# Seven mixer projections of a fused two-model block as split high and low products, with three weight slots instead of four

## The chip, the cores and the metric

The kernel runs on one core of a Trainium2 chip. The metric is the device time of one execution in microseconds (us). The program is written engine by engine: each engine has an instruction stream of its own, executes it strictly in order, and meets the others only through semaphores.

## The reference

The reference computes, for 256 tokens of width 1024, one block with a mixer and a retrieval layer, and then a two-layer model on its result. Only the start of it matters here:

```python
h = _rmsnorm(x, norm1_g[l])
p = h @ w_in[l]
(gq, gk, gv, gz, ga, gb, mq, mk, mv, mo, mi, mf) = jnp.split(p, offsets, axis=-1)
y_a = _gdn_group(gq, gk, gv, gz, ga, gb, conv_w[l], gdn_a_log[l], gdn_dt_bias[l], gdn_norm_g[l])
y_b = _mlstm_group(mq, mk, mv, mo, mi, mf, mlstm_i_bias[l], mlstm_f_bias[l], mlstm_norm_g[l])
```

`h @ w_in` is a 256 x 1024 by 1024 x 4128 product in float32. Its 4096 columns beside the gates are eight blocks of 512: the queries, keys and values of the gated delta rule (`gq`, `gk`, `gv`, which go through a five-tap convolution and a SiLU, and the first two through a normalisation), its output gate, and the queries, keys, values and output gate of the mLSTM. The delta rule inverts a triangular matrix per 128 tokens, head and direction. After the block comes a retrieval layer that gathers rows of two tables, and then a second model with modulated norms; the modulation (`ada`) is a product of one conditioning vector with a 50 MB matrix.

## The kernel before

**Projections.** The eight column blocks are called `proj(0)` to `proj(7)`, in the order keys, values, queries of the delta rule, then mLSTM values, mLSTM queries, mLSTM keys, delta-rule gate, mLSTM gate. Each has a weight block `("in", n)` of 1024 x 512 (2 MB, `slots[i]`, [128, 4096]). The normalised input lies transposed in `hT` ([128, 8, 256]: eight chunks of the width, 256 tokens). A projection is two groups `g`, each filling one PSUM bank of 512 columns; a group is two accumulations of eight matmuls of 128x128 by 128x256, except `proj(3)`, where it is one accumulation of eight matmuls with 512 columns and the tokens as output rows. Operands are float32. The profile shows each such float32 matmul as two records, so a projection of 32 matmuls stands there as 64, and `proj(3)` with 16 as 32.

**The order on TensorE** is written out by hand: gates, `proj(0)`, the cumulated gates (`cum`, and after a wait for VectorE's `v_cc` their transposes `crow`), `proj(1)`, `em`, `proj(2)`, `l2(1,0)` (sums of squares of the keys), `decays(0)`, `decays(1)`, `l2_rows(1,0)` (waits for `v_rq`), `proj(3)`, `decays(2)`, `decays(3)`, the key products `kk`, `proj(4)`, `l2(0,1)`, `tokens(0)`, `l2_rows(0,1)`, `proj(5)`, the query products `kq` with two steps of `cond` between, `proj(6)`, `tokens(1)`, `proj(7)`, then for four heads a step of `cond` and four transposes `dd`, and then `level(1..6)`, each level with eight steps, and behind each step one of `cond` and one of `mlstm`.

**PSUM** is a ring of seven banks. `take(name, reader, n)` waits until the bank's last reader is done. So `proj(4)` waits for `v_at0` 3, VectorE's product in `decays(2)`, and `tokens(0)` waits for `v_kk` 1, VectorE's first product with `kk`.

**The order on VectorE**: normalised input, gates (`v_gl`), cumulated gates (`v_cc`), `v_crow` and scans (`v_rows`), `conv(1,0)` (16 multiply-adds), `em`, `conv(2,1)`, `l2_root(1,0)`, `decays(0)`, `decays(1)`, `l2(1,0)`, `conv(0,2)`, `decays(2)`, `decays(3)`, `l2_root(0,1)`, four `kk` products, `l2(0,1)`, four `kq` products, four first blocks of `DT`.

**The order on ScalarE**: gates (`a_gl`), `evac(0)` (the copy of a projection out of PSUM, one for each group), the exponentials `a_eg`, `conv(1,0)` (four first taps), `conv_out(1,0)` (SiLU), `squares(1,0)`, `evac(1)`, `a_em`, `conv(2,1)`, `conv_out(2,1)`, `evac(2)`, `roots(1,0)`, `decays(0)`, `decays(1)`, `conv(0,2)`, `evac(3)`, `conv_out(0,2)`, `squares(0,1)`, `decays(2)`, `decays(3)`, `evac(4)`, `roots(0,1)`, `tokens(0)`, `evac(5)`, `evac(6)`, `tokens(1)`, `evac(7)`. In every function the engine waits for its own result (`seq`, `told`) before the next instruction.

**GpSimd** masks the matrices `AM` by levels (`level(l)`), from `v_kk` and `v_l2` 4 on.

**Loads.** SyncE issues all of them in program order. `load(name, until, ...)` takes the next slot of a ring, waits until its last user (`until`) is done, and issues. Four slots are in use at this stage: three of `wring` and `wring3`. The eight `("in", n)` blocks take slots 0 to 3 twice. Sixteen blocks `("ada", i)` of 2 MB follow in the same ring, each read by two steps of `cond`.

**The same split elsewhere.** The two-layer model at the end already multiplies in rounded high parts and low parts: ScalarE copies a [128, 2048] piece of weights to float32r (`wh`), VectorE subtracts (`wl`), and TensorE issues three float32r matmuls (`hh`x`wh`, `hl`x`wh`, `hh`x`wl`) for each float32 one.

Of the kernel before, what the change touches and what calls it, by code (L numbers as in the profile page):

```python
# [91 lines left out]
def program(nc, a, out):  # L92
# [11 lines left out]
        "p_cu": ("p_mb", 8), "p_cd": ("p_dec", 8), "p_dn": ("p_cd", 24), "p_ckv": ("p_ms", 4), "p_hs": ("p_ckv", 3),  # L104
        "p_vt": ("p_lb", 24), "p_s": ("p_cu", 22), "p_pt": ("p_q", 10), "p_o": ("p_sc", 10), "p_y": ("p_o", 8),
        "p_hb": ("p_wo", 4), "p_hr": ("p_pl", 4), "p_wd": ("p_crs", 3), "p_mrs": ("p_wd", 4),
        "v_gu": ("v_gps", 1), "v_ge": ("v_gu", 1), "v_gl": ("v_ge", 1), "v_cum": ("v_gl", 1), "v_cc": ("v_cum", 1),
        "v_crow": ("v_cc", 1), "v_rows": ("v_crow", 1), "v_em": ("v_rows", 1), "v_h2": ("v_em", 1),
        "v_pq": ("v_kk", 4),
        "a_gp": ("a_c16", 1), "a_gl": ("a_gp", 1), "a_eg": ("a_gl", 1), "a_em": ("a_eg", 1), "a_h2T": ("a_em", 1), "a_xc": ("a_h2T", 4),  # L110
# [14 lines left out]
    def at(name, n):  # L125

        sem = S[name]
        while name in GOES_ON:
            name, before = GOES_ON[name]
            n += before  # L130
        return sem, n

    def sb(name, n, stack=ctx, p=128):
        return stack.enter_context(nc.sbuf_tensor(name, [p, n], F32))
# [17 lines left out]
    g2b = cl[:, 0:1024]  # L152
    vec = sb("vec", NVEC)
    mods = [sb("mods0", 96), sb("mods1", 96)]
    wring = sb("wring", 3 * 4096)
    gt = sb("gt", 340)[:, :]
    ss = sb("ss", 8)[:, :]
    st = sb("st", 48)
# [8 lines left out]
    wt = sb("wt", 128)[:, :]  # L167
    cvb = [sb(f"cvb{i}", 512)[:, :].rearrange("p (i n) -> p i n", i=2) for i in range(2)]
    early = ExitStack()
    arena = sb("arena", 29760, early)  # L170
    wring3 = sb("wring3", 4096, early)
    slots = [wring[:, 4096 * i:4096 * i + 4096] for i in range(3)] + [wring3[:, :]]
# [19 lines left out]
    def flat(ap):  # L192
        return ap.rearrange("p m n -> p (m n)")

    def heads4(buf, h):
        return buf[:, 4 * h:4 * h + 4, :]
# [17 lines left out]
    tmp1 = area(MARK + 2048, 1024)  # L214
    gsum = tmp1[:, 0:256]
    sqt = flat(OT).rearrange("p (b n) -> p b n", b=8)
    rq = flat(DD)[:, 0:16]
    raw2 = area(4096, 2048).rearrange("p (m n) -> p m n", m=16)
    OTs = [OT, raw2]
    X, BV, VN, KD, S1 = ET, AM, DD, ET, ET[:, 8:16, :]  # L220
    QT, KT = qkv[:, 0:4, :], qkv[:, 4:8, :]
    PTs = [area(2048 + 512 * i, 512) for i in range(4)]
# [109 lines left out]
    def mem(stack, name, n):  # L332
        return stack.enter_context(nc.sbuf_tensor(name, [128, n], F32))

    def cols(t):
        return t[:, :].rearrange("p (c n) -> p c n", n=256)

    yo_, xT_, sqb_ = mem(ctx, "yo", 2048), mem(ctx, "xT", 2048), mem(ctx, "sqb", 2048)
    xT, sqb = cols(xT_), cols(sqb_)
    whl = [(mem(ctx, f"wh{i}", 2048), mem(ctx, f"wl{i}", 2048)) for i in range(3)]  # L340
# [103 lines left out]
    def norm_at(t):  # L444


        return [st[:, 32 + 5 * t + i:33 + 5 * t + i] for i in range(5)]

    def both_cols(b):
        return b[:, 0:256], b[:, 256:512]  # L450

# [57 lines left out]
    def _(sp):  # L509
        free, count, nth = [None] * 4, [0] * 4, [0]  # L510

        def load(name, until, *parts, n=4):

            i = nth[0] % n
            nth[0] += 1
            for signal in free[i] or ():
                sp.wait_ge(*at(*signal))
            for put, src in parts:
                sp.dma_start(put(slots[i]), src).then_inc(S[f"d_w{i}"], 16)  # L519
                count[i] += 16  # L520
            free[i] = until if isinstance(until, list) else [until]
            ready[name] = S[f"d_w{i}"], count[i], slots[i]

        def kcols(w, c0, n):
            return ((lambda ap: ap[:, 0:8 * n].rearrange("p (k c) -> p k c", k=8)),
                    w[:, c0:c0 + n].rearrange("(k p) c -> p k c", p=128))
# [23 lines left out]
        sp.dma_start(wgate, a["gates"]).then_inc(S["d_g"], 16)  # L550
        w_in = a["w_in"][0]
        for n, c0 in enumerate((512, 1024, 0, 3088, 2064, 2576, 1536, 3600)):
            load(("in", n), ("p_pj", 2 * n + 2), kcols(w_in, c0, 512))
            if n == 0:
                sp.dma_start(cbase[:, 128:1688], a["c_base"][:, 128:1688]).then_inc(S["d_c"], 16)
            if n == 2:
                sp.dma_start(cl[:, :], a["c_levels"]).then_inc(S["d_l"], 16)
        for i in range(LOADS_EARLY):
            load(("ada", i), ("p_ada", i + 1), (lambda ap: ap, a["ada"][i]))
        for half in range(2):  # L560
            load(("wo", half), ("p_wo", OUT_LAST.index((half, 1)) + 1), kcols(a["w_out"][0], 512 * half, 512))
        load(("wq", 0), ("p_q", 4), kcols(a["peer_wq"][0], 0, 512))
        nth[0] = 0
        sp.wait_ge(*at("g_lev", 28))
        sp.dma_start(g2b, a["norm2_g"][0].partition_broadcast(128)).then_inc(S["d_g2"], 16)
# [47 lines left out]
    def _(pe):  # L613
# [17 lines left out]
        def weights(name):  # L631
            s, n, ap = ready[name]
            pe.wait_ge(s, n)
            return ap

        def mm(o, l, r, start, stop):
            return pe.matmul(o, l, r, start=start, stop=stop)  # L637
# [5 lines left out]
        def c128(i):  # L643
            return slice(128 * i, 128 * i + 128)
# [22 lines left out]
        k.then_inc(S["p_g"], 1)  # L667

        def proj(n):
            w = weights(("in", n)).rearrange("p (k c) -> p k c", k=8)  # L670
            for g in range(2):
                b = take(("pj", 2 * n + g), "a_pj", 2 * n + g + 1)
                if n == 3:
                    for kk in range(8):
                        k = mm(b, hT[:, kk, c128(g)], w[:, kk, :], kk == 0, kk == 7)
                else:
                    for i in range(2):
                        for kk in range(8):
                            k = mm(b[:, 256 * i:256 * i + 256], w[:, kk, c128(2 * g + i)], hT[:, kk, :], kk == 0, kk == 7)
                k.then_inc(S["p_pj"], 1)  # L680

        proj(0)
# [104 lines left out]
        pe.wait_ge(*at("a_c16", 1))  # L787
        cond = conditioning(range(GROUPS_EARLY), sc32, "p_ada", 1)
        pe.wait_ge(*at("v_l2", 4))
        for h in range(4):  # L790
            if h < 2:
                next(cond)
            b = take(("kq", h), "v_pq", h + 1)
            for t in range(2):
                k = mm(b[:, c128(t)], KT[:, h, c128(t)], QT[:, h, c128(t)], True, True)
            k.then_inc(S["p_kq"], 1)
        proj(6)
        pe.wait_ge(*at("a_conv", 2))
        tokens(1, 8)
        proj(7)  # L800
# [558 lines left out]
    def _(ve):  # L1359
# [8 lines left out]
        def told(ins, name, n):  # L1368

            ins.then_inc(S[name], 1)  # L1370
            ve.wait_ge(*at(name, n))

        def tt(o, x, y, op):
            return ve.tensor_tensor(o, x, y, op)  # L1374

        def ts(o, x, s1, s2, op0, op1):
            return ve.tensor_scalar(o, x, s1, s2, op0, op1)  # L1377
# [37 lines left out]
        seq(stt(GL, GU, 0.0, GE, MAX, ADD))  # L1415
        seq(stt(GL[:, :, 0:8], GL[:, :, 0:8], -1.0, bc(na, 2, 1), MUL, MUL))
        told(ts(GL[:, :, 8:16], GL[:, :, 8:16], -1.0, None, MUL, BYP), "v_gl", 1)
        ve.wait_ge(*at("p_cum", 1))
        b = where["cum"]
        seq(ve.tensor_copy(by_dir(Gc), b[:, 0:16].rearrange("p (d t h) -> p d t h", d=2, t=2)))  # L1420
# [21 lines left out]
        def conv(g, n):  # L1442
            ve.wait_ge(*at("a_tap", n + 1))
            for blk in range(4 * g, 4 * g + 4):
                for j in range(1, 5):
                    w = vcol("convw", 5 * blk + j)
                    k = stt(qkv[:, blk, :], raw[:, blk, j:j + 256], w, qkv[:, blk, :], MUL, ADD)
                    if j < 4 or blk < 4 * g + 3:
                        seq(k)
            told(k, "v_conv", n + 1)  # L1450
# [8 lines left out]
        def l2_root(g, n):  # L1459
            ve.wait_ge(*at("a_l2", n + 1))  # L1460
            told(ve.reciprocal(rq[:, 8 * g:8 * g + 8], rq[:, 8 * g:8 * g + 8]), "v_rq", n + 1)

        def pairs(ap):
            return ap.rearrange("p (d t) n -> p d (t n)", d=2)

        conv(1, 0)
        ve.wait_ge(*at("p_em", 1))
        for d in range(2):
            i = tt(by_dir(EM)[:, d], where["em"][:, 16 * d:16 * d + 16].rearrange("p (t c) -> p t c", t=2)[:, :, 4 * d:4 * d + 4],
                   by_time(Fc)[:, :, 4 * d:4 * d + 4], SUB)  # L1470
        told(i, "v_em", 1)
        conv(2, 1)
        l2_root(1, 0)
        decays(0)
        decays(1)
        l2(1, 0)
        conv(0, 2)
        decays(2)
        decays(3)
        l2_root(0, 1)  # L1480
        for h in range(4):
            ve.wait_ge(*at("p_kk", h + 1))
# [565 lines left out]
    def _(ac):  # L2048
# [16 lines left out]
        def copy(o, x):  # L2065
            return ac.activation(o, x, ACT.Copy)  # L2066
# [639 lines left out]
```

## Time and profile before

| what | value |
|---|---|
| median of 3 runs | 1764.28 us (1759.52 to 1766.96) |
| the profiled execution | 1777.99 us, its span 1776.2 us |
| granted TensorE clock over the span | 0.936 |
| TensorE matmuls, weight loads | 1530.4 us busy (86%), 1118.8 us (63%) |
| VectorE, ScalarE, GpSimd | 1055.2 us (59%), 526.8 us (30%), 791.2 us (45%) |
| chain that ended last | PE 57%, DVE 11%, POOL 11%, DMA 10%, issue 6%, ACT 3% |

The profiled execution is one run with the profiler on. Busy shares are means over stages with very different limits; the projections occupy the first 167 us of the 1776. A row of a timeline gives start, duration, engine, line, operation, operands and count, and in brackets the idle time before it and what ended that idle time.

### The profile page before, as it was taken

The page shows a single profiled execution, that of the slowest core. Times are in us where ns is not written, and L with a number is a line of the kernel's source. Part 1 is how long each engine was busy: PE and PEld are TensorE (multiplying, and loading weights), DVE is VectorE, ACT ScalarE, POOL GpSimd, SP SyncE. Part 2 cuts the span into 40 slices and gives each one's busy share as a digit, 9 for nine tenths or more (in the row PEclk, how much of TensorE's full clock was granted, in tenths as well). Part 3 has the DMA queues.
Part 4 walks back from the last instruction along what each step waited for, and adds up shares of the span by engine and source line. Part 5 has one row for each costly group of instructions (what it writes and reads, how often), then busy time and mean ns, then how long its engine had stood idle before and what let it go on. Part 6 is the DMA issues. An engine that isn't in the chain of part 4 may idle for free.

```text
span 1776.2 us, 22879 instructions
## 1 busy us (share of the span) xinstructions
PE 1530.4 (86%) x8778; PEld 1118.8 (63%) x8778; DVE 1055.2 (59%) x2105; ACT 526.8 (30%) x768; POOL 791.2 (45%) x746
## 2 busy tenths in 40 slices
PE   7999879976666679999788886788999998999999
PEld 6787557665321136666443432328999985699999
DVE  2511445479858768777766664507776435567754
ACT  3422211121112113222200001127554442566642
POOL 0023213037676777656666777751654110215530
PEclk9999998998778889999989998898999989999999
DMA  8224754069899999999999999996555425735550
GB/s 311 96 95 187 315 200 165 24 233 351 295 398 402 397 386 365 393 393 391 402 403 407 397 360 397 409 369 197 183 186 181 175 96 209 265 128 186 176 191 35
DMA packets 188573, 477.20 MB, mean 269 GB/s; under 512 B 10544, under 2 KB 80432, under 8 KB 185264
## 3 DMA queue, kind: packets, MB, share of 16 engines
q0 software_dynamic: 73728, 268.47, 39.1%
q1 hardware_dynamic: 114736, 207.27, 32.9%
q8 instruction: 70, 1.15, 0.3%
q14 instruction: 39, 0.32, 0.0%
HBM read 474.65 MB, written 1.05 MB: 268 GB/s over the span
## 4 chain that ended last, share of the span: by engine, by line
PE 57%; DVE 11%; POOL 11%; DMA 10%; issue 6%; ACT 3%; SPq 2%; another core or an unknown queue 1%; ACTq 0%; DVEq 0%; POOLq 0%
PE ps L637 56%; POOL arena L2638 9%; DMA arena<-in_peer_v,cl 6%; DVE arena L1735 2%; DVE arena L1374 2%; DMA wring<-in_ffn_w_up 2%; POOL wring L2638 2%; SPq L519 2%; DMA wring<-in_ada 1%; PE ps L641 1%; DVE arena L1380 1%; DVE arena L1377 1%; DVE wring L1735 1%; ACT L2063 1%; ACT arena L2063 1%
## 5 line engine op out<-in xcount | busy, mean ns | idle before, releaser
L637 PE MATMUL ps<-arena,wring 128*128 128x256 f32 (+2 forms) x2744 | 685.8, 474 | 118.3 <-DMA arena<-in_peer_v,cl 87.0
L637 PEld LDWEIGHTS ps<-arena,wring 128*128 128x128 f32 (+1 forms) x2744 | 403.7, 171 | 380.2 <-issue 172.8
L2638 POOL DMA_INDIRECT arena<-in_peer_u,arena x214 | 238.6, 1115 | 207.6 <-DVE arena L1693 83.6
L1735 DVE CUSTOM_DVE_ANT_0 arena<-arena 128x1024 f32<-128x1024 f32 x214 | 256.7, 1225 | 123.6 <-DMA arena<-in_peer_u,arena 102.3
L2638 POOL DMA_INDIRECT arena<-in_peer_v,cl x214 | 223.9, 1046 | 77.7 <-issue 62.3
L2063 ACT ACT_TABLE_LOAD x65 | 83.4, 1283 | 418.1 <-DVE arena L1735 173.2
L637 PE MATMUL ps<-hh,wh 128*128 128x256 f32 x704 | 201.2, 286 | 3.9 <-DVE hl L1380 3.9
L1374 DVE TENSOR_TENSOR wl<-wring,wh 128x2048 fp32r<-128x2048 f32 (+1 forms) x76 | 167.8, 2208 | 60.5 <-ACT wh L2066 58.6
L637 PE MATMUL ps<-hl,wh 128*128 128x256 f32 x704 | 200.5, 285 | 0.0
L637 PE MATMUL ps<-hh,wl 128*128 128x256 f32 x704 | 200.4, 285 | 0.0
L1380 DVE SCALAR_TENSOR_TENSOR cvb<-ps,vec,cvb 128x255 f32<-128x255 f32 x264 | 127.4, 483 | 107.5 <-ACT cvb L2063 100.2
L2066 ACT ACTIVATE wh<-wring 128x2048 fp32r<-128x2048 f32 x78 | 146.1, 1873 | 76.8 <-PE ps L637 75.0
L637 PE MATMUL ps<-arena 128*128 128x128 f32 (+4 forms) x868 | 123.6, 305 | 37.1 <-DVE arena L1374 19.9
L637 PEld LDWEIGHTS ps<-arena 128*128 128x128 f32 (+1 forms) x868 | 110.2, 203 | 71.5 <-issue 28.5
L2592 POOL TENSOR_TENSOR arena<-arena,cl 128x256 f32<-128x256 f32 x56 | 41.9, 748 | 230.4 <-DVE arena L1380 120.4
L2656 POOL TENSOR_TENSOR cvb<-cvb 128x256 f32<-128x256 f32 x44 | 96.7, 2198 | 106.2 <-ACT cvb L2063 106.2
L637 PEld LDWEIGHTS ps<-hh,wh 128*128 128x128 f32 x704 | 136.5, 194 | 4.7 <-issue 4.4
L637 PEld LDWEIGHTS ps<-hl,wh 128*128 128x128 f32 x704 | 136.6, 194 | 0.0
L637 PEld LDWEIGHTS ps<-hh,wl 128*128 128x128 f32 x704 | 136.5, 194 | 0.0
L2063 ACT ACTIVATE cvb<-ps,vec 128x256 f32<-128x256 f32 x132 | 74.6, 565 | 177.2 <-PE ps L637 139.9
L1374 DVE TENSOR_TENSOR arena<-arena,ps 128x512 f32<-128x512 f32 x68 | 46.5, 687 | 118.4 <-PE ps L637 109.5
L2066 ACT ACTIVATE arena<-ps 128x512 f32<-128x512 f32 (+1 forms) x77 | 44.1, 572 | 191.9 <-PE ps L637 165.0
(243 smaller groups left out, 2079.3 us busy)
## 6 DMA issues: line engine op xcount, KB each, us to landing
wring<-in_ffn_w_up SPq DMA_DIRECT2D x66, 1024.0 KB
wring<-in_ada SPq DMA_DIRECT2D x24, 2048.0 KB, 7.7
wring<-in_ffn_w_down SPq DMA_DIRECT2D x12, 2048.0 KB
wring<-in_w_in SPq DMA_DIRECT2D x8, 2048.0 KB, 13.0
wring<-in_ffn_w_down SPq DMA_DIRECT2D x6, 1536.0 KB
wring<-in_peer_wq SPq DMA_DIRECT2D x4, 2048.0 KB
wring<-in_attn_w_qkv SPq DMA_DIRECT2D x4, 2048.0 KB
wring<-in_w_out SPq DMA_DIRECT2D x2, 2048.0 KB
```

The source lines that it names most:

```text
L519: sp.dma_start(put(slots[i]), src).then_inc(S[f"d_w{i}"], 16)
L637: return pe.matmul(o, l, r, start=start, stop=stop)
L641: return pe.transpose(o, i, ident[0:n, 0:n])
L1374: return ve.tensor_tensor(o, x, y, op)
L1377: return ve.tensor_scalar(o, x, s1, s2, op0, op1)
L1380: return ve.scalar_tensor_tensor(o, x, s, y, op0, op1)
L1735: ve.tensor_tensor_reduce(out=o, in0=o, in1=h2[:, t, :], scale=1.0, scalar=0.0, op0=MUL, op1=ADD, accum_out=dots[j % 2][:, k:k + 1]).then_ ...
L2063: return ac.activation(o, x, f, bias=bias, scale=scale, accum_out=accum)
L2066: return ac.activation(o, x, ACT.Copy)
L2592: k = po.tensor_tensor(OTs[l % 2][:, m:m + 2, :], AM[:, m:m + 2, :], bc(cl[:, o:o + 128], 2, 1), MUL)
L2638: po.indirect_dma_start(out=ring[n % NR], out_offset=None, in_=table, in_offset=bass.IndirectOffsetOnAxis(ap=which, axis=0)).then_inc(S[f" ...
L2656: seq(po.tensor_tensor(cv[:, 0, :], cv[:, 0, :], cv[:, 1, :], MUL))
```

## The change

`proj(1)` to `proj(7)` are computed as three float32r products: high part of the weights times high part of `h`, and the two mixed products. A projection is cut into two pieces of [128, 2048] (256 columns of weights). ScalarE copies piece `p` rounded to float32r into one of four buffers `wh_in[p % 4]` (`hi_in`), VectorE subtracts and writes the low part over the loaded weights (`lo_in`), and TensorE waits for `v_wl` p+1. The rounded copy waits until the piece four before it has been used (`in_used`). ScalarE also makes `hTh` from `hT`, VectorE writes `hTl` over `hT`, after `proj(0)` has read it. The four buffers lie in `wring3` (two) and in the areas of `DT` and `PQ`; `hTh` lies in `DD`, and `rq` moves from there to `st`. The weight blocks now turn in three slots. The `ada` blocks go to slots `(2 + i) % 4`, and slot 3 is free for them only after `p_pj` 16, the end of `proj(7)`. On TensorE `proj(6)` moves ahead of the `kq` products. The diff without the lines that only move buffers:

```diff
+    split = ExitStack()
+    wl_in = [mem(split, f"il{i}", 4096) for i in range(3)]
+    mem(split, "pad0", 2048)
+    hTl = cols(mem(split, "hTl", 2048))
+    mem(split, "pad1", MARK)
+    wh_pq = cols(mem(split, "ih3", 2048))
+    mem(split, "pad2", 2048)
+    hTh = cols(mem(split, "hTh", 2048))
+    wh_dt = cols(mem(split, "ih2", 2048))
+    mem(split, "pad3", 8)
+    wh_in = [cols(mem(split, "ih0", 2048)), cols(mem(split, "ih1", 2048)), wh_dt, wh_pq]
...
+    def in_used(p):
+        return 8 if p in (4, 5) else p + 3
+
+    def in_piece(p):
+        n = 1 + p // 2
+        part = slice(256 * (p % 2), 256 * (p % 2) + 256)
+        return ("in", n), ready["in", n][2].rearrange("p (k c) -> p k c", k=8)[:, :, part], wl_in[n % 3][:, :].rearrange("p (k c) -> p k c", k=8)[:, :, part]
...
@@ SyncE
-            load(("in", n), ("p_pj", 2 * n + 2), kcols(w_in, c0, 512))
+            load(("in", n), ("p_pj", 2 * n + 2), kcols(w_in, c0, 512), n=3)
...
+        free[3] = [("p_pj", 16)]
         for i in range(LOADS_EARLY):
-            load(("ada", i), ("p_ada", i + 1), (lambda ap: ap, a["ada"][i]))
+            load(("ada", i), ("p_ada", i + 1), (lambda ap: ap, a["ada"][i]), slot=(2 + i) % 4)
         for half in range(2):
-            load(("wo", half), ...)
-        load(("wq", 0), ("p_q", 4), kcols(a["peer_wq"][0], 0, 512))
+            load(("wo", half), ..., slot=2 - 2 * half)
+        load(("wq", 0), ("p_q", 4), kcols(a["peer_wq"][0], 0, 512), slot=1)
@@ TensorE
+        def proj3(n):
+            h = hTh.bitcast(FR), hTl.bitcast(FR)
             for g in range(2):
                 b = take(("pj", 2 * n + g), "a_pj", 2 * n + g + 1)
+                for i in range(2):
+                    p = 2 * n - 2 + (i if n == 3 else g)
+                    pe.wait_ge(*at("v_wl", p + 1))
+                    w = wh_in[p % 4].bitcast(FR), in_piece(p)[2].bitcast(FR)
                     for kk in range(8):
+                        for x, y in ((0, 0), (0, 1), (1, 0)):
+                            if n == 3:
+                                left, right = h[x][:, kk, c128(g)], w[y][:, kk, :]
+                            else:
+                                left, right = w[x][:, kk, c128(i)], h[y][:, kk, :]
+                            k = mm(b[:, 256 * i:256 * i + 256], left, right, kk == x == y == 0, kk == 7 and x == 1)
                 k.then_inc(S["p_pj"], 1)
...
         pe.wait_ge(*at("v_l2", 4))
+        proj(6)
         for h in range(4):
...
-        proj(6)
         pe.wait_ge(*at("a_conv", 2))
@@ VectorE
         told(ts(GL[:, :, 8:16], GL[:, :, 8:16], -1.0, None, MUL, BYP), "v_gl", 1)
+        def lo_in(n):
+            for p in range(2 * n - 2, 2 * n):
+                ve.wait_ge(*at("a_wh", p + 1))
+                name, w, low = in_piece(p)
+                told(tt(low.bitcast(FR), w, wh_in[p % 4], SUB), "v_wl", p + 1)
+
+        ve.wait_ge(*at("p_pj", 2))
+        ve.wait_ge(*at("a_wh", 1))
+        seq(tt(hTl.bitcast(FR), hT, hTh, SUB))
+        lo_in(1)
         ve.wait_ge(*at("p_cum", 1))
...
+        lo_in(2)
         conv(1, 0)
...
         told(i, "v_em", 1)
+        lo_in(3)
         conv(2, 1)
         l2_root(1, 0)
+        lo_in(4)
         decays(0)
         decays(1)
         l2(1, 0)
         conv(0, 2)
+        lo_in(5)
         decays(2)
         decays(3)
...
+        lo_in(6)
         l2(0, 1)
+        lo_in(7)
@@ ScalarE
+        def hi_in(n):
+            for p in range(2 * n - 2, 2 * n):
+                name, w, low = in_piece(p)
+                ac.wait_ge(*ready[name][0:2])
+                if p > 3:
+                    ac.wait_ge(*at("p_pj", in_used(p - 4)))
+                told(copy(wh_in[p % 4].bitcast(FR), w), "a_wh", p + 1)
+
+        ac.wait_ge(*at("v_hT", 4))
+        seq(copy(hTh.bitcast(FR), hT))
+        hi_in(1)
         evac(0)
         ac.wait_ge(*at("v_cc", 1))
         seq(actf(EG, Gc, ACT.Exp))
         told(actf(GT, GT, ACT.Exp), "a_eg", 1)
+        hi_in(2)
         conv(1, 0)
         conv_out(1, 0)
         squares(1, 0)
         evac(1)
         ac.wait_ge(*at("v_em", 1))
         told(actf(EM, EM, ACT.Exp), "a_em", 1)
+        hi_in(3)
         conv(2, 1)
         conv_out(2, 1)
         evac(2)
+        hi_in(4)
         roots(1, 0)
...
         evac(3)
+        hi_in(5)
...
         evac(4)
+        hi_in(6)
         roots(0, 1)
         tokens(0, ktok)
         evac(5)
+        hi_in(7)
         evac(6)
```

## Rows read from the trace of the kernel before

**Rows 1.** The page, part 1: busy time, share of span and count per engine.

```profile
PE 1530.4 (86%) x8778; PEld 1118.8 (63%) x8778; DVE 1055.2 (59%) x2105; ACT 526.8 (30%) x768; POOL 791.2 (45%) x746
```

**Rows 2.** Timeline of TensorE, 0 to 180 us: start, duration, engine, line, operation.

```profile
16.55 16.54 PE L637 MATMUL ps<-arena,wring 128*128 128x256 f32 x64
...
37.52 16.22 PE L637 MATMUL ps<-arena,wring 128*128 128x256 f32 x64
...
73.29 1.95 PE L637 MATMUL ps<-cbase,arena 128*128 128x128 f32 x16
75.08 13.90 PE L637 MATMUL ps<-wring,arena 128*128 128x512 f32 x32
...
96.00 14.05 PE L637 MATMUL ps<-arena,wring 128*128 128x256 f32 x64 [1.66 <-DVE arena L1374]
...
114.45 1.97 PE L641 MATMUL ps<-cbase,arena 128*128 128x128 f32 x8 [2.73 <-DVE arena L1374]
...
119.63 14.45 PE L637 MATMUL ps<-arena,wring 128*128 128x256 f32 x64
...
152.77 13.98 PE L637 MATMUL ps<-arena,wring 128*128 128x256 f32 x64
...
174.29 1.07 PE L637 MATMUL ps<-wring,rsb 128*32 128x512 f32 x8 [0.32 <-DMA wring<-in_ada]
```

**Rows 3.** Window of `proj(6)`: stretch, length, busy (count) per engine, clock, DMA share.

```profile
138.00:152.00 14.00, 14.00 (x68) 12.30 (x67) 5.56 (x7) 1.88 (x2) 11.65 (x15) 1.00 0.19 80
```

**Rows 4.** Two windows of float32r matmuls in the last model.

```profile
1232.00:1240.00 8.00, 8.00 (x69) 8.00 (x69) 6.21 (x6) 6.45 (x7) 0.56 (x2) 1.00 0.02 5
...
1226.00:1230.00 4.00, 3.91 (x18) 3.94 (x19) 3.44 (x8) 3.53 (x8) 1.47 (x2) 0.51 1.10 354
```

**Rows 5.** Tile `wh`: the same split elsewhere, durations in ns minimum/median/maximum.

```profile
L2066 ACT ACTIVATE wh<-wring x78: 1058/1917/1923, 1211.7 to 1756.3; 128x2048 fp32r<-128x2048 f32 x74, 128x1024 fp32r<-128x1024 f32 x4
L1374 DVE TENSOR_TENSOR wl<-wring,wh x76: 1224/2292/2293, 1215.2 to 1757.4; 128x2048 fp32r<-128x2048 f32 x70, 128x1024 fp32r<-128x1024 f32 x6
```

**Rows 6.** Timeline of VectorE, 33 to 120 us.

```profile
36.90 0.18 DVE L1424 COPY gt<-gt 128x16 f32<-128x16 f32 x1
...
41.55 8.29 DVE L1380 SCALAR_TENSOR_TENSOR arena<-arena,vec 128x256 f32<-128x256 f32 x16
...
72.38 0.20 DVE L1461 RECIPROCAL arena<-arena 128x8 f32<-128x8 f32 x1 [5.37 <-ACT arena L2063]
...
79.22 1.41 DVE L1380 SCALAR_TENSOR_TENSOR arena<-arena,ps 128x512 f32<-128x512 f32 x2
80.68 8.30 DVE L1380 SCALAR_TENSOR_TENSOR arena<-arena,vec 128x256 f32<-128x256 f32 x16
89.98 1.13 DVE L1377 TENSOR_SCALAR arena<-ps,gt 128x128 f32<-128x128 f32 x4 [1.00 <-PE ps L637]
95.16 0.69 DVE L1374 TENSOR_TENSOR arena<-arena,ps 128x512 f32<-128x512 f32 x1 [4.05 <-ACT arena L2063]
...
113.71 2.85 DVE L1374 TENSOR_TENSOR arena<-arena,ps 128x512 f32<-128x512 f32 x4
```

**Rows 7.** Timeline of ScalarE, 37 to 95 us.

```profile
38.95 2.13 ACT L2063 ACTIVATE arena<-arena,vec 128x256 f32<-128x256 f32 x4
49.93 1.28 ACT L2063 ACT_TABLE_LOAD   x1 [8.85 <-DVE arena L1380]
...
53.40 1.23 ACT L2066 ACTIVATE arena<-ps 128x512 f32<-128x512 f32 x2
...
70.71 1.28 ACT L2063 ACT_TABLE_LOAD   x1
...
93.15 1.28 ACT L2063 ACT_TABLE_LOAD   x1
```

**Rows 8.** Timeline of SyncE's queue, 160 to 172 us.

```profile
166.78 2.94 SPq L519 DMA_DIRECT2D wring<-in_ada  x3
```

**Rows 9.** Window of the three `ada` loads in flight, columns as in Rows 3; GB/s last.

```profile
166.60:182.00 15.40, 13.72 (x97) 6.83 (x96) 1.55 (x3) 6.81 (x11) 4.07 (x6) 1.00 0.95 387
```

More of the change, by code:

```diff
@@ L106, in program @@
         "p_hb": ("p_wo", 4), "p_hr": ("p_pl", 4), "p_wd": ("p_crs", 3), "p_mrs": ("p_wd", 4),
-        "v_gu": ("v_gps", 1), "v_ge": ("v_gu", 1), "v_gl": ("v_ge", 1), "v_cum": ("v_gl", 1), "v_cc": ("v_cum", 1),
+        "v_gu": ("v_gps", 1), "v_ge": ("v_gu", 1), "v_gl": ("v_ge", 1), "v_wl": ("v_hT", 4), "v_cum": ("v_gl", 1), "v_cc": ("v_cum", 1),
         "v_crow": ("v_cc", 1), "v_rows": ("v_crow", 1), "v_em": ("v_rows", 1), "v_h2": ("v_em", 1),
@@ L154, in program @@
     mods = [sb("mods0", 96), sb("mods1", 96)]
-    wring = sb("wring", 3 * 4096)
     gt = sb("gt", 340)[:, :]
@@ L169, in program @@
     early = ExitStack()
+    wring = sb("wring", 3 * 4096, early)
     arena = sb("arena", 29760, early)
@@ L216, in program @@
     sqt = flat(OT).rearrange("p (b n) -> p b n", b=8)
-    rq = flat(DD)[:, 0:16]
+    rq = st[:, 0:16]
     raw2 = area(4096, 2048).rearrange("p (m n) -> p m n", m=16)
@@ L336, in cols @@
         return t[:, :].rearrange("p (c n) -> p c n", n=256)
+    split = ExitStack()
[9 more added lines that the diff above has]
+    wh_in = [cols(mem(split, "ih0", 2048)), cols(mem(split, "ih1", 2048)), wh_dt, wh_pq]
+    split.close()
+    mem(ctx, "wring_stays", 3 * 4096)
     yo_, xT_, sqb_ = mem(ctx, "yo", 2048), mem(ctx, "xT", 2048), mem(ctx, "sqb", 2048)
@@ L510, in _, with load @@
         free, count, nth = [None] * 4, [0] * 4, [0]
-        def load(name, until, *parts, n=4):
-            i = nth[0] % n
+        def load(name, until, *parts, n=4, slot=None):
+            i = nth[0] % n if slot is None else slot
             nth[0] += 1
@@ L557, in _ @@
                 sp.dma_start(cl[:, :], a["c_levels"]).then_inc(S["d_l"], 16)
+        free[3] = [("p_pj", 16)]
         for i in range(LOADS_EARLY):
-            load(("ada", i), ("p_ada", i + 1), (lambda ap: ap, a["ada"][i]))
+            load(("ada", i), ("p_ada", i + 1), (lambda ap: ap, a["ada"][i]), slot=(2 + i) % 4)
         for half in range(2):
-            load(("wo", half), ("p_wo", OUT_LAST.index((half, 1)) + 1), kcols(a["w_out"][0], 512 * half, 512))
-        load(("wq", 0), ("p_q", 4), kcols(a["peer_wq"][0], 0, 512))
+            load(("wo", half), ("p_wo", OUT_LAST.index((half, 1)) + 1), kcols(a["w_out"][0], 512 * half, 512), slot=2 - 2 * half)
+        load(("wq", 0), ("p_q", 4), kcols(a["peer_wq"][0], 0, 512), slot=1)
         nth[0] = 0
@@ L669, in proj @@
         def proj(n):
-            w = weights(("in", n)).rearrange("p (k c) -> p k c", k=8)
+            if n > 0:
+                return proj3(n)
+            w = weights(("in", 0)).rearrange("p (k c) -> p k c", k=8)
+            for g in range(2):
+                b = take(("pj", g), "a_pj", g + 1)
+                for i in range(2):
+                    for kk in range(8):
+                        k = mm(b[:, 256 * i:256 * i + 256], w[:, kk, c128(2 * g + i)], hT[:, kk, :], kk == 0, kk == 7)
+                k.then_inc(S["p_pj"], 1)
+        def proj3(n):
+            h = hTh.bitcast(FR), hTl.bitcast(FR)
             for g in range(2):
                 b = take(("pj", 2 * n + g), "a_pj", 2 * n + g + 1)
-                if n == 3:
+                for i in range(2):
+                    p = 2 * n - 2 + (i if n == 3 else g)
+                    pe.wait_ge(*at("v_wl", p + 1))
+                    w = wh_in[p % 4].bitcast(FR), in_piece(p)[2].bitcast(FR)
                     for kk in range(8):
[L675 to L679, printed above, removed]
+                        for x, y in ((0, 0), (0, 1), (1, 0)):
[4 more added lines that the diff above has]
+                            k = mm(b[:, 256 * i:256 * i + 256], left, right, kk == x == y == 0, kk == 7 and x == 1)
                 k.then_inc(S["p_pj"], 1)
```

## The prediction

> **What bounds the kernel now.** I read the page's busy shares first: TensorE stands at 86% [rows 1], an average over stages. So I went to its timeline over the first 180 us [rows 2], where every edit of the change lies. The reader is to see there that the projections run back to back, with two short waits for VectorE: 1.66 us ahead of `proj(4)` and 2.73 us ahead of `tokens(0)`. The stage is bound by TensorE, but hardly more than by the chain VectorE-ScalarE: `l2_rows(1,0)` starts at 73.29 [rows 2], and the reciprocal it waits for is done at 72.6 [rows 6]. Next come the timelines of VectorE and ScalarE [rows 6, 7]: few busy microseconds, but in one chain, in which each hands to the other, and each executes in order. Last, the loads: the step of `cond` at 174.29 waits 0.32 us for an `ada` block that was asked for when `proj(7)` ended at 166.8 [rows 2, 8]. After 174 us all work hangs on this chain (levels, output, retrieval, last model), and I see nothing between that would take up a delay, so a shift here is a shift of the end.
>
> **TensorE's gain.** A projection now takes 13.9 to 14.45 us, and `proj(1)` 16.22 [rows 2]; the two projections without a row took 14.08 and 13.98; together the seven take 100.6 us. The new one has 2 groups x 2 x 8 x 3 = 96 float32r matmuls of 256 columns, in `proj(3)` too. In the last model 69 such matmuls stand in a window of 8 us, two of them cut by its edges, so one takes 0.12 us; at half clock 18 stand in 4 us, so 0.22 us [rows 4]. 96 x 0.12 = 11.6 us, seven make 81. The gain is 19.6 us, if nothing comes late. A stretch of about 4 us at half clock costs some 2 us.
>
> **The new work.** For each of 14 pieces ScalarE copies [128, 2048] in 1.92 us and VectorE subtracts in 2.29 us; the same forms stand in the trace [rows 5]. With 0.04 us from one instruction to the next a `hi_in` is 3.9 us and a `lo_in` 4.65 us; `hTh` and `hTl` add one each. ScalarE gets 28.8 us, VectorE 34.4 us. Both sat idle for more than that in these 167 us. But the new instructions stand in order ahead of links of the chain, so I follow the chain and ask at each link which of the two engines is late.
>
> 1. `hTl` needs the end of `proj(0)` at 33.1 [rows 2]. Then `hTl` and two pieces: 33.2 + 3 x 2.33 = 40.1. Only then do the five small operations on `cum` follow (1.04 us; the last now ends at 37.1 [rows 6]): `v_cc` at 41.2, 4.1 us late. TensorE, done with `cum` at 36, waits for it ahead of `crow` and `proj(1)`, and goes cold.
> 2. VectorE's scans end at 41.5 + 4.1, `lo_in(2)` follows: `conv(1,0)` starts at 50.3 instead of 41.55 [rows 6]. ScalarE's side is earlier: `a_eg` at 43.0, `hi_in(2)` 3.9, taps 2.1 [rows 7], 49.0. `conv(1,0)` ends at 58.6.
> 3. ScalarE: SiLU and squares 3.45 (49.93 to 53.40), `evac(1)` 1.25 [rows 7], `a_em` 1.5: 64.85. `hi_in(3)` gives its pieces at 66.8 and 68.7, the taps are done at 70.9; VectorE, idle since 59, subtracts until 71.4 and runs `conv(2,1)` for 8.3 until 79.8. Before it ended at 67.0.
> 4. ScalarE: SiLU 2.4, `evac(2)` 1.25, `hi_in(4)` 3.9, `roots` 1.6 (load at 70.71 to the reciprocal at 72.38 [rows 6, 7]): 88.9, reciprocal 89.15. TensorE has been idle since about 73 and starts `l2_rows(1,0)` at 89.2 instead of 73.29: 15.9 us late. It starts cold: 3.6 us for `l2_rows`, then 11.6, so `proj(3)` ends at 104.3.
> 5. VectorE: `lo_in(4)` to 93.8, `decays(0)` and `(1)` 6.6 (72.6 to 79.2), `l2` 1.45, `conv(0,2)` 8.3 [rows 6]: 110.15. `lo_in(5)` (its pieces are ready at 108.8) to 114.8. `decays(2)`: 1.13, then from the table load to the end of the product 2.7 (93.15 to 95.85) [rows 6, 7]: 118.65. The PSUM bank of `proj(4)` is free then: it starts at 118.7 instead of 96.00 [rows 2], 22.7 us late. Cold: 13.5 us, to 132.2.
> 6. ScalarE: last half of `evac(4)` 0.6, `hi_in(6)` 3.9, `roots` 1.6: 138.35; VectorE: reciprocal and first `kk` product (0.7 each [rows 6]): 139.3. `tokens(0)` starts 24.8 us late, the worst point.
> 7. From here TensorE is the late one again: 5.2 us to `proj(5)` as before, 11.6 to 156.1; `proj(6)` (pieces at 146) to 167.7; `kq` with its two steps 4.1, `tokens(1)` 0.9; `proj(7)` to 184.3. `lo_in(7)` waits for `evac(5)` and is done near 163. Before, `proj(7)` ended at 166.75 [rows 2]: 17.6 us late. Moving `proj(6)` ahead of `kq` frees `PQ` and `DT` and costs nothing by itself: GpSimd's `PQ` masks come later, but are done by about 178.
>
> All of this is 19.6 us won and 37 us lost to waits.
>
> **The loads.** `("in", n)` in three slots: block n+3 is asked for at the end of `proj(n)` and needed a projection later or more; 7.5 us (166.8 to 174.3 [rows 2, 8]) are covered. The `ada` blocks are not. Before, blocks 0, 1 and 2 came while projections ran, and only block 3 was asked for at the end of `proj(7)`. Now block 1 is for slot 3, free at `p_pj` 16, and SyncE holds blocks 2 and 3 behind this wait. So at 184.3 three blocks of 2.1 MB are asked for together: the first lands 7.5 us later, the others at 387 GB/s [rows 9], 5.3 us apart. Block 3 is there 18 us after `proj(7)`, against 7.5: 10.4 us more, and its step of `cond` stands in TensorE's order ahead of the mLSTM and the levels. It goes from 174.29 to about 202.3: 28 us late. The next blocks then arrive faster than they are used. What this costs at least is 6.4 us (block 1 lands after 7.5, the four `dd` steps follow at 1.6 each, and block 3 is no hindrance), at most 17 (the three share the engines and land together at 18, then the four steps). I take 10.4, the rate of rows 9. `wo` and `wq` get other slots, each one `ada` block later, still ahead of their use.
>
> The Trainium skill (DMA: Bandwidth & Descriptors, Queues, rings and completion order) says that on each DMA engine the descriptors of one queue are consumed in ring order; by that block 1 lands first, and the sum stands; no row here separates the three.
>
> Bounds of the rest: two cold starts could be missing, or two more follow the stall (2 us each); the subtractions beside GpSimd's masks could take half as long again, 2 us. Sum: +28, from +18 to +39. On the profiled execution's 1778.0 that is 1806; it lies 13.7 above the median of the runs, and on the median of 1764.3 it is 1792.
>
> **Rivals.**
> - *TensorE stays the bound* and the other two keep up, because they were idle for two thirds of the stage. Then -19.6, +4.1 for `v_cc`, and +10.4 for the loads: 1759; without the loads' part 1749. For it: the shares in rows 1. Against it: the waits that exist already, with no extra work, in rows 2. It decides if `l2_rows(1,0)` starts before 74. The Trainium skill (Perfetto Trace Analysis, Identifying the Most-Contended Engine) tells one to improve the most contended engine, and to judge TensorE by the share of weight loads; these stand at 12.30 of 14.00 us in `proj(6)` [rows 3]. By that rule the change should help.
> - *The loads are hidden*: the stall shrinks because levels would have waited anyway. +17.6: 1782. Against it: steps 1 to 4 of the levels followed at once after 174.29.
> - *The three blocks land together*: 17.6 + 17 = +35, 1799. For it: three issues one behind the other on one queue [rows 8].
> - *The chain is longer than I follow it*, a bank or a table load more: about +39, 1803.
>
> **Numbers.** Forecast (+23 to +31) 0.62, TensorE stays the bound 0.12, loads hidden 0.13, land together 0.08, longer chain 0.05. A measurement of this kernel can tell 0.5%, 8.8 us, from no change. The first rival is half within it (1759), half faster (1749). So faster 0.07, same 0.07, slower 0.86. Range 1777 to 1803; a split run would most likely stand at 1787 to 1796.
>
> **What would show it.** Right: `crow` near 41, `l2_rows(1,0)` near 89 after an idle of 15 us, `proj(4)` near 119, `proj(7)` ending near 184, the first `ada` step behind it 7 us later and the step of block 3 near 202, projections of 11.6 us where warm. Wrong: projections back to back; matmuls slower than 0.12 us when warm; a copy or subtraction away from 1.92 and 2.29 us; or a gap later in the kernel that closes by 20 us.

## The result, and the profile after

The changed kernel takes 1789.4 us (median of 4 runs, 1785.5 to 1794.6) against 1765.5 us before (4 runs): a ratio of 1.0144, interval 1.0106 to 1.0182. It is 23.9 us slower (19 to 32 by the interval), where 28 were forecast; 1789.4 lies inside the range, 2.6 us below the predicted 1792.

The page of the changed kernel, part 1, answers to [rows 1]: TensorE is 10 us less busy, VectorE 36 us more, ScalarE 29 us more.

```profile
PE 1520.8 (85%) x9034; PEld 1126.1 (63%) x9034; DVE 1091.6 (61%) x2120; ACT 555.5 (31%) x783; POOL 795.9 (44%) x746
```

TensorE's timeline, changed kernel (start, duration, operation, idle before), answers to [rows 2]:

```profile
41.01 0.59 PE L668 MATMUL ps<-cbase,gt 128*8 128x128 f32 x2 [5.59 <-DVE gt L1479]
...
89.19 3.76 PE L664 MATMUL ps<-cbase,st 128*128 128x128 f32 x16 [17.71 <-DVE st L1516]
...
116.08 1.22 PE L664 MATMUL ps<-arena 128*128 128x128 f32 x4 [6.91 <-DVE arena L1420]
118.86 0.58 PE L664 MATMUL ps<-hTh,ih 128*128 128x256 f32 x1 [1.56 <-DVE arena L1417]
...
139.59 1.97 PE L668 MATMUL ps<-cbase,arena 128*128 128x128 f32 x8 [5.56 <-DVE arena L1417]
...
190.97 1.94 PE L664 MATMUL ps<-wring,rsb 128*32 128x512 f32 x8 [7.43 <-DMA wring<-in_ada]
...
200.75 1.06 PE L664 MATMUL ps<-wring,rsb 128*32 128x512 f32 x8 [0.52 <-DMA wring<-in_ada]
```

All rows but the third are the six stations of the forecast: `crow`, `l2_rows(1,0)`, `proj(4)`, `tokens(0)`, the first step of `ada` block 1 and the first step of block 3. The third is the last of the key products `kk`. The waits ahead of `crow`, `l2_rows(1,0)`, `tokens(0)` and block 1's step were 1.2, 0, 2.7 and 0 us before; now they are 5.6, 17.7, 5.6 and 7.4 us. Ahead of `proj(4)` the new wait is the 6.9 us in front of `kk`. The releaser in the brackets names the culprit: VectorE each time, and at the `ada` step a load.

VectorE's timeline of the changed kernel, answers to [rows 6]:

```profile
35.26 4.62 DVE L1417 TENSOR_TENSOR il<-wring,ih 128x2048 fp32r<-128x2048 f32 x2
...
50.07 8.30 DVE L1423 SCALAR_TENSOR_TENSOR arena<-arena,vec 128x256 f32<-128x256 f32 x16
...
66.73 4.62 DVE L1417 TENSOR_TENSOR il<-wring,ih 128x2048 fp32r<-128x2048 f32 x2 [8.08 <-ACT ih L2127]
71.39 8.30 DVE L1423 SCALAR_TENSOR_TENSOR arena<-arena,vec 128x256 f32<-128x256 f32 x16
88.94 0.20 DVE L1516 RECIPROCAL st<-st 128x8 f32<-128x8 f32 x1 [9.25 <-ACT st L2124]
89.17 4.62 DVE L1417 TENSOR_TENSOR il<-wring,ih 128x2048 fp32r<-128x2048 f32 x2
...
110.25 4.62 DVE L1417 TENSOR_TENSOR il<-wring,ih 128x2048 fp32r<-128x2048 f32 x2
```

ScalarE's, answers to [rows 7]. Between the first taps of `conv(2,1)` and their result it waits; the copies stand behind `evac(2)`, with `roots` behind them:

```profile
68.61 2.13 ACT L2124 ACTIVATE arena<-arena,vec 128x256 f32<-128x256 f32 x4
79.76 1.28 ACT L2124 ACT_TABLE_LOAD   x1 [9.02 <-DVE arena L1423]
81.06 1.06 ACT L2124 ACTIVATE arena<-arena 128x1024 f32<-128x1024 f32 x1
82.14 1.23 ACT L2127 ACTIVATE arena<-ps 128x512 f32<-128x512 f32 x2
83.40 3.85 ACT L2127 ACTIVATE ih<-wring 128x2048 fp32r<-128x2048 f32 x2
87.27 1.28 ACT L2124 ACT_TABLE_LOAD   x1
```

Both timelines show the loss in small: VectorE with 36 us more work was idle for 8.1 and 9.3 us, and ScalarE with 29 us more for 9.0 us in between, each waiting for the other, with the new work ahead of what the other waited for. Next come the new instructions by tile (min/median/max ns), and a window of TensorE in `proj(7)` at full clock (1.00). The window counts 97 float32r matmuls in 11.2 us, some of them cut by its edges. By their starts (191 intervals from 144.32 to 166.91 in `proj(5)` and `proj(6)`) one takes 0.118 us. This answers to [rows 4, 5].

```profile
L2127 ACT ACTIVATE ih<-wring x14: 1909/1910/1920, 24.6 to 158.6; 128x2048 fp32r<-128x2048 f32 x14
L1417 DVE TENSOR_TENSOR il<-wring,ih x14: 2291/2292/2834, 35.3 to 161.5; 128x2048 fp32r<-128x2048 f32 x14
```

```profile
172.20:183.40 11.20, 11.20 (x97) 11.14 (x95) 4.60 (x5) 2.77 (x4) 10.24 (x13) 1.00 0.01 2
```

**Where the total is measured.** The two profiled spans differ by 16.5 us only (1776.2 and 1792.7). The reader should not take that for the effect. GpSimd's first gather of the retrieval layer is a mark behind all that was changed. Its row in the kernel before and in the changed one (timeline of GpSimd):

```profile
380.86 1.14 POOL L2638 DMA_INDIRECT arena<-in_peer_u,arena  x1 [83.59 <-DVE arena L1693]
```

```profile
404.32 1.14 POOL L2717 DMA_INDIRECT arena<-in_peer_u,arena  x1 [82.61 <-DVE arena L1754]
```

At this mark the shift is 23.5 us, as in the medians (23.9). From there to the last model's first norm it is 829.5 us in the profile of before and 819.0 in that of after, and 817 to 820 in the profiles of the first four experiments below. In the four later ones, on other chips, it is 823 to 835. So this stage varies by itself, and the profile of before had a slow one; its 10.5 us more are most of the 13.7 us by which it lay above its median.

### The profile page after: what moved, and what is told of

The parts are those of the page before. It is cut to its first block, busy times and chain, and to the rows that moved or that the text cites. A ratio compares the mean times of both kernels' runs of the same rounds, so it can differ in the third digit from the quotient of the medians.

```text
span 1792.7 us, 23458 instructions
## 1 busy us (share of the span) xinstructions
PE 1520.8 (85%) x9034; PEld 1126.1 (63%) x9034; DVE 1091.6 (61%) x2120; ACT 555.5 (31%) x783; POOL 795.9 (44%) x746
## 4 chain that ended last, share of the span: by engine, by line
PE 55%; DMA 14%; DVE 10%; POOL 9%; issue 4%; ACT 1%; SPq 0%; DVEq 0%; ACTq 0%; POOLq 0%
PE ps L664 54%; DMA arena<-in_peer_v,cl 8%; POOL arena L2717 8%; DMA wring<-in_ffn_w_up 2%; DVE arena L1796 2%; DVE arena L1417 2%; DMA wring<-in_ada 1%; POOL wring L2717 1%; DMA wring<-in_peer_v,cl 1%; PE ps L668 1%; DVE arena L1423 1%; DVE arena L1420 1%; DMA wring<-in_peer_u,arena 1%; DVE arena L1726 0%; DVE wring L1796 0%
## 5 line engine op out<-in xcount | busy, mean ns | idle before, releaser
L664 PE MATMUL ps<-arena,wring 128*128 128x256 f32 (+2 forms) x2360 | 599.5, 492 | 106.0 <-DMA arena<-in_peer_v,cl 99.3
L664 PEld LDWEIGHTS ps<-arena,wring 128*128 128x128 f32 (+1 forms) x2360 | 331.0, 167 | 356.3 <-DMA arena<-in_peer_v,cl 178.2
L2717 POOL DMA_INDIRECT arena<-in_peer_u,arena x214 | 246.9, 1154 | 197.3 <-DVE arena L1754 82.6
L2671 POOL TENSOR_TENSOR arena<-arena,cl 128x256 f32<-128x256 f32 x56 | 45.7, 816 | 249.1 <-DVE arena L1423 147.5
```

Source lines behind the costliest of these rows:

```text
L2671: k = po.tensor_tensor(OTs[l % 2][:, m:m + 2, :], AM[:, m:m + 2, :], bc(cl[:, o:o + 128], 2, 1), MUL)
L2717: po.indirect_dma_start(out=ring[n % NR], out_offset=None, in_=table, in_offset=bass.IndirectOffsetOnAxis(ap=which, axis=0)).then_inc(S[f" ...
```

## The experiments

### Only the order of the `ada` slots

```diff
-            load(("ada", i), ..., slot=(2 + i) % 4)
+            load(("ada", i), ..., slot=(2, 0, 1, 3)[i % 4])
```

> The changed kernel with one edit: the ada blocks turn in slots 2, 0, 1, 3 instead of 2, 3, 0, 1, so that only block 3 waits for the end of proj(7), and block 1 is asked for at the end of proj(6), block 2 at the end of proj(7). My theory (the stall behind proj(7) is the wait for block 1, held back by slot 3): proj(7) still ends at 183.6 us; the two steps of block 1 follow at once; block 2 lands 7.4 us after proj(7), block 3 about 5 us behind it; the first step of block 3 goes from 200.75 to about 196.3, 4.5 us earlier, and the kernel ends about 4.5 us earlier (1785 on the median of 1789.4). Rival (the stall is bandwidth, the three blocks come as fast as they can): no change.

Measured: 1787.3 us, ratio to the kernel before 1.0134 (1.0103 to 1.0165). TensorE's timeline of this run:

```profile
183.77 1.06 PE L664 MATMUL ps<-wring,rsb 128*32 128x512 f32 x8
...
191.19 1.07 PE L664 MATMUL ps<-wring,rsb 128*32 128x512 f32 x8 [4.19 <-DMA wring<-in_ada]
...
196.77 1.06 PE L664 MATMUL ps<-wring,rsb 128*32 128x512 f32 x8
```

Block 1 is there, block 2 comes 7.4 us behind `proj(7)`, block 3's step is at 196.8, 4.0 us earlier, where 4.5 were expected. The first gather is at 401.1, 3.2 us earlier. The total moved by 2 us, which the intervals can't tell from nothing or from 4. So by the trace the stall depends on which block is held back, as expected; that the 4 us reach the end is not shown.

### One product instead of three in `proj(1)` to `proj(3)`

```diff
-                        for x, y in ((0, 0), (0, 1), (1, 0)):
+                        for x, y in (((0, 0),) if n < 4 else ((0, 0), (0, 1), (1, 0))):
```

> The changed kernel with proj(1), proj(2) and proj(3) as one product (high times high) instead of three; the low parts of these three are computed but not multiplied, so their mixed products are missing from the result. ScalarE and VectorE do all they did. It takes 3 x 64 matmuls of 0.12 us = 23 us from TensorE. My theory (up to proj(4) the chain ScalarE-VectorE sets the pace): l2_rows(1,0) still starts near 89, proj(4) near 118.8, the end of proj(7) near 183.6, all within 1 us, total the same as the changed kernel (1789). Rival (TensorE's own work sets the pace in this stage too): proj(4) and all behind it 8 to 23 us earlier, total 1767 to 1781.

Measured: 1791.8 us, ratio to before 1.0163 (1.0131 to 1.0195). TensorE's timeline of this run:

```profile
89.72 3.79 PE L664 MATMUL ps<-cbase,st 128*128 128x128 f32 x16 [18.20 <-DVE st L1516]
...
116.59 1.23 PE L664 MATMUL ps<-arena 128*128 128x128 f32 x4 [12.22 <-DVE arena L1420]
...
119.37 0.58 PE L664 MATMUL ps<-hTh,ih 128*128 128x256 f32 x1 [1.55 <-DVE arena L1417]
```

By the estimate of the expectation 23 us of matmuls are gone, and `proj(4)` starts half a microsecond later than with them (119.4 against 118.9). The waits take up the time; the one before 116.6 is 12.2 us against 6.9. Up to `proj(4)` TensorE's own work is free; the rival is out.

### The loads alone, in float32

The kernel before with the change's three weight slots, its `ada`, `w_out` and `wq` slots, and `proj(6)` ahead of `kq`.

```diff
+            load(("in", n), ..., n=3)
+        free[3] = [("p_pj", 16)]
+            load(("ada", i), ..., slot=(2 + i) % 4)
```

> The kernel before, in float32, with only the change's slots (weights in three, ada blocks in (2+i)%4 with slot 3 free at the end of proj(7), w_out and wq blocks as in the change) and proj(6) ahead of the kq products. My theory: the projections end as before (166.7), the first step of ada block 1 waits 7.4 us behind, the first step of block 3 is about 9.5 us later than the 174.3 of the kernel before, total +9.5 us (1775 on a median of 1765.5). Rival (the stall costs nothing of its own, because TensorE or others would have waited anyway): within 2 us of the kernel before.

Measured: 1773.1 us against 1765.0, ratio 1.0060 (1.0038 to 1.0083). TensorE's timeline of this run:

```profile
172.01 1.93 PE L638 MATMUL ps<-wring,rsb 128*32 128x512 f32 x8 [7.80 <-DMA wring<-in_ada]
...
181.98 1.06 PE L638 MATMUL ps<-wring,rsb 128*32 128x512 f32 x8
```

`proj(7)` ends at 164.2, 2.5 us earlier than in [rows 2], where the same end was expected; the granted clock up to there was 0.99 against 0.96 in the profile of before. Block 3's step follows 17.8 us behind, against 7.6 in [rows 2], and it no longer waits for a load: the steps behind block 1, of which the first two ran at half clock (1.93 us for 1.06), come last. So the slots alone cost 10.6 us by the ratio (6.7 to 14.7; 8.0 by the medians) of the change's 24, with no copy or product in them.

### The same work in other places

```diff
@@ ScalarE
-        hi_in(3)
         conv(2, 1)
+        hi_in(3)
...
         evac(2)
-        hi_in(4)
         roots(1, 0)
         decays(0)
         decays(1)
         conv(0, 2)
+        hi_in(4)
@@ VectorE
-        lo_in(3)
         conv(2, 1)
+        lo_in(3)
         l2_root(1, 0)
-        lo_in(4)
         decays(0)
         decays(1)
         l2(1, 0)
         conv(0, 2)
-        lo_in(5)
+        lo_in(4)
         decays(2)
         decays(3)
+        lo_in(5)
```

(`hi_in(5)` goes behind `decays(3)`, `hi_in(6)` behind `roots(0,1)`.)

> The changed kernel with the same work in other places: ScalarE makes hi_in(3) behind the taps of conv(2,1), hi_in(4) behind the taps of conv(0,2), hi_in(5) behind decays(3), hi_in(6) behind roots(0,1); VectorE makes lo_in(3) behind conv(2,1), lo_in(4) behind conv(0,2), lo_in(5) behind decays(3). Theory (not the 63 us of copies and subtractions cost time, but their places ahead of links of the chain): l2_rows(1,0) starts at 80.7 instead of 89.0, proj(4) at 105.6 instead of 118.8, proj(7) ends at 167 instead of 183.6; total about 16 us below the changed kernel (1773). Rival (the two engines have too much work for this stage, wherever it stands): less than 5 us gained.

Measured: 1774.3 us, ratio to before 1.0047 (1.0030 to 1.0065): 15 us less than the changed kernel, with every copy, subtraction and product in it. TensorE's timeline of this run:

```profile
80.56 3.78 PE L664 MATMUL ps<-cbase,st 128*128 128x128 f32 x16 [9.55 <-DVE st L1516]
...
105.56 0.40 PE L664 MATMUL ps<-hTh,ih 128*128 128x256 f32 x1 [2.07 <-DVE arena L1417]
...
123.07 1.97 PE L668 MATMUL ps<-cbase,arena 128*128 128x128 f32 x8 [2.72 <-DVE arena L1417]
...
173.82 1.94 PE L664 MATMUL ps<-wring,rsb 128*32 128x512 f32 x8 [7.37 <-DMA wring<-in_ada]
...
183.59 1.06 PE L664 MATMUL ps<-wring,rsb 128*32 128x512 f32 x8 [0.76 <-DMA wring<-in_ada]
```

`l2_rows(1,0)` at 80.6, `proj(4)` at 105.6, end of `proj(7)` 7.4 us before 173.8, at 166.45: each within 0.6 us of what was expected. The projections now end where those of the kernel before did (166.7), and the load stall is what is left on top.

### Places and slots together

> The run e4_placed together with the ada slot order of e1_ada_order. Theory (the two losses, places and loads, are separate and add): proj(7) ends at 166.4 as in e4, the first step of ada block 3 about 4 us earlier than the 183.6 of e4, total 1771, 6 us above the kernel before; what stays is v_cc late by 4, two late subtractions, and block 2 behind the end of proj(7). Rival (what one gives, the other takes back): 1774 as e4.

The edit is that of the first and the fourth experiment. Measured on another chip, on which the kernel before takes 1780.3 us: ratio 1.0023 (1.0005 to 1.0041), so 4 us above before, where 6 were expected. Block 3's step is at 181.5, 2.1 us before that of the fourth experiment, where 4 were expected. But `proj(7)` ended at 168.2 in this run, 1.7 us later than there (166.4 expected); measured from that end the step comes 13.3 us behind, against 17.1, which is 3.8 us less. The wait for block 2 is 4.4 us where the wait for block 1 was 7.4. So by the traces the two losses are separate and add. The totals can't show it: the intervals of this run and of the fourth experiment overlap.

### Only the last three projections

In this version `proj(0)` to `proj(4)` stay float32, four weight slots stay, and no load is held back. The high parts need three buffers, which lie in `DT`, `PQ` and in 1024 columns each of `raw` and `vtok`; so `tokens(1)` moves behind `proj(7)` and the first `DT` blocks behind its end.

```diff
@@ VectorE
         decays(3)
+        for p in (8, 9, 10):
+            lo_in(p)
+        ve.wait_ge(*at("p_pj", 10))
+        seq(tt(hTl.bitcast(FR), hT, hTh, SUB))
         l2_root(0, 1)
...
         l2(0, 1)
+        lo_in(11)
...
+        lo_in(12)
+        lo_in(13)
@@ ScalarE
         decays(3)
+        for p in (8, 9, 10):
+            hi_in(p)
         evac(4)
...
+        hi_in(11)
         evac(5)
+        hi_in(12)
         evac(6)
+        hi_in(13)
```

> The kernel before with only proj(5), proj(6) and proj(7) split into three products; proj(0) to proj(4), the four weight slots and the ada slots as before. The high parts lie in DT, PQ and in two free halves (the end of raw and vtok); ScalarE and VectorE make the first three pieces and hTl behind decays(3), where VectorE sat idle for 15 us, the other three between the evacuations; tokens(1) moves behind proj(7). Theory (the products are worth 2.4 us a projection if the copies and subtractions stand where their engines wait anyway and no load is held back): l2_rows(0,1) starts as before (116), proj(5) to proj(7) take 11.6 us each, no wait for ada at the end of proj(7), the first gather about 7.5 us earlier than in the kernel before, total -7.5 us (1757.5 on a median of 1765). Rival (any 26 us more on the two engines show somewhere in this stage): at or above 1765.

Measured: ratio 0.9928 (0.9905 to 0.9950), 1767.0 against 1780.3 us. VectorE's timeline of this run: behind the new work the reciprocal still waits for ScalarE, now 1.0 us where it was 15.0 in the kernel before. `tokens(0)`, which hangs on it, starts at 112.5, and in the control below at 112.6, so the new work fits into the wait.

```profile
97.87 2.29 DVE L1426 TENSOR_TENSOR il<-wring,ihd 128x2048 fp32r<-128x2048 f32 x1 [1.27 <-ACT ihd L2137]
...
108.25 2.29 DVE L1426 TENSOR_TENSOR hTl<-arena,hTh 128x2048 fp32r<-128x2048 f32 x1 [3.24 <-PE ps L673]
111.56 0.20 DVE L1513 RECIPROCAL st<-st 128x8 f32<-128x8 f32 x1 [1.02 <-ACT st L2134]
```

This version beats both kernels. But it gained 12.8 us (9 to 17) where the products are worth 7.5. So the control, which moves `tokens(1)` and the `DT` blocks alone, and the version once more beside it, on one chip:

> The control of e5_last_three: the kernel before, all in float32 with no copies or subtractions, with only what e5 moves: tokens(1) behind proj(7) on TensorE and ScalarE, and the first blocks of DT behind the end of proj(7). e5 came out 0.72% below the kernel before (interval 0.50 to 0.95), where its products were worth 0.43%. Theory A (the moves are free and neutral; the rest of e5's gain is TensorE's clock or chance): ratio 1.000, within 0.25%. Theory B (the moves give something, for example because GpSimd's masks no longer run beside VectorE's DT blocks): 0.2 to 0.4% below the kernel before, and the way from block 3's step to the first gather 3 us shorter than the 206.6 of the kernel before, without a colder clock there.

> The kernel of e5_last_three once more, beside its control e7_order_only on one chip. Theory A: its distance from e7 is the 7.6 us of the products plus up to 2 us of cold clock around l2_rows(0,1), so a ratio to the kernel before of 0.995 to 0.9965. Theory B: again 0.993, with e7 at 0.997.

Measured: the control 1.0008 (0.9989 to 1.0028), the version 0.9940 (0.9919 to 0.9960), 1766.2 against 1775.7 us. The moves give nothing, and theory B is out: the stretch it wanted 3 us shorter took 207.8 us in the control; the second ratio is just below the range that theory A gave (0.995 to 0.9965), with an interval that reaches into it. Where the rest above the 7.5 us comes from is not shown. The two profiles of this chip do not contain it: block 3's step is at 165.6 against 170.6 in the control, and the first gather at 373.1 against 378.4, some 5 us.

## Why the prediction was right

**The gain.** 96 matmuls at 0.12 us, 11.6 us a projection: measured 0.118, 11.4 us where warm. Right.

**Steps 1 to 6, the chain.** Forecast against measured start: `crow` 41.2 and 41.0, `conv(1,0)` 50.3 and 50.1, `lo_in(3)` 66.8 and 66.7, the reciprocal 88.9 and 88.9, `l2_rows(1,0)` 89.2 and 89.2, `proj(4)` 118.7 and 118.9, `tokens(0)` 139.3 and 139.6. Durations of the new instructions came from rows with the same form [rows 5]; what decided was to walk the two orders in parallel and take the later engine at each link. The idle time ahead of `l2_rows(1,0)` was 17.7 us instead of 15, because TensorE was done at 71.5 and not at 73; that cost nothing. The prediction's "two short waits" left out the 1.2 us ahead of `crow`. That the chain, and not TensorE, sets the pace here was argued in the prediction and is shown by the one-product run; that it is the places and not the amount of work is shown by the fourth.

**Step 7.** `proj(7)` ended at 183.5 for 184.3. `lo_in(7)` ran beside GpSimd's masks and took 5.59 us for 4.65 (the 2834 ns in the row of `il`), off the chain, within the bound given.

**The loads.** Block 1 7.4 us behind `proj(7)` (7.5 forecast), block 3's step 17.2 behind it (18). That is 9.6 us for 10.4; the float32 run has 10.2 by its trace and 10.6 (6.7 to 14.7) in time. The Trainium skill (DMA: Bandwidth & Descriptors, Queues, rings and completion order) has descriptors consumed in ring order, and the trace agrees: block 1 lands first, 7.4 us after its issue, as block 0 did, which was asked for alone at 155.9. Not three but four blocks were asked for together, at 183.6, 184.0, 184.4 and 184.9; they landed 7.4, 11.9, 16.3 and 20.7 us after their issues, 4.9 us apart, where the prediction had 5.3 from the 387 GB/s of [rows 9]. The rival in which all three land together is out. That the landing of block 3 decides is right only by half a microsecond, though, and this closeness was luck: TensorE waited 0.52 us for it, behind steps of which the first ran at half clock and the second in part (1.94 and 1.69 us for 1.06; granted 0.50 from 191 to 194 us and 0.70 from 194 to 196). The prediction's lower bound of 6.4 us, block 3 no hindrance, left these slow steps out, and a group of matmuls of 1.06 us behind the `dd` steps; without a wait for block 3 the stall would have been 9.1 us, not 6.4.

**Where it was off.** The forecast was +28, the medians say +23.9, with an interval (19 to 32) that contains 28. At block 3's step the shift is 26.5 us: 0.8 less than forecast from the projections and 0.8 from the loads. At the first gather it is 23.5. The stretch between the two took 206.6 us in the profile of before and 203.6 in that of the change. These 3 us are the clock's and not slack that closed: the profiler counts 1185 matmul records there in both, busy for 179.7 us at a granted clock of 0.94 and for 176.4 us at 0.96. It varies as much within one kernel: the version with the last three projections was profiled twice, on two chips, with 202.3 us (busy 175.1, clock 0.97) and 207.5 us (busy 181.1, clock 0.93) for this stretch. So "a shift here is a shift of the end" stands, as far as one profile against another can tell, which is some 3 to 5 us.

The stated bounds do not quite come out of their terms. Two missing cold starts and the lower price of the loads give +20, not +18; two more cold starts, the slower subtractions and the higher price give +41, not +39. The result lies well inside either.

**The rivals.** "TensorE stays the bound" rested on the busy shares and on the rule to improve the most contended engine, which the Trainium skill gives (Perfetto Trace Analysis, Identifying the Most-Contended Engine). The change did relieve TensorE, by 10 us, and the kernel got 24 us slower: here the rule, taken by shares over the span, points the wrong way. Taken for the stretch from `proj(5)` to `proj(7)`, where TensorE never waits, it holds: there the same products gain.

## What to carry to other kernels

VectorE and ScalarE were idle for two thirds of this stage, and still had room only at places where no other engine was soon to wait for what stands behind. So new work goes behind what another engine waits for; the same instructions moved by a few lines were worth 15 us here. Where memory for a new buffer is taken from a ring of loads, follow the loads behind it in the issuing queue: one slot that came free two projections later held back its own load and those behind it, and cost some 10 us. Split only those products in whose stretch the multiplying engine does not wait.

## What the runs showed of the hardware

The stretch around `l2_rows(0,1)` ran at half clock for longer in the profile of before than in that of the control, which ran on another chip with the same order of work ahead of it (granted clock from 105 to 125 us 0.83 and 0.91): `l2_rows(0,1)` takes 3.62 us and `proj(5)` 14.45 [rows 2] there, against 2.54 and 13.98 in the control (timeline of TensorE):

```profile
112.64 1.97 PE L641 MATMUL ps<-cbase,arena 128*128 128x128 f32 x8 [2.73 <-DVE arena L1374]
114.40 2.54 PE L637 MATMUL ps<-cbase,arena 128*128 128x128 f32 x16
116.78 13.98 PE L637 MATMUL ps<-arena,wring 128*128 128x256 f32 x64
```

So two executions of the same work can differ by 1.5 us per such place, and a term of that size can't be read off a single profile. Over a longer stretch the difference grows: with the same kernel and the same 1185 matmul records, on two chips, the way from block 3's step to the first gather took 202.3 us in one profile and 207.5 in another (granted clock 0.97 and 0.93).

Four loads of 2 MB asked for within 1.4 us on one queue landed one after the other, the first after 7.4 us like one on its own, each further one 4.9 us later.
